# Expert outputs added by indirect DMA into a DRAM table of token sums, the last block applied on TensorE, and the second expert's rows gathered behind the first layer

## What is computed

```python
def moe_ffn(h, router_w, router_b, w1, b1, w2, b2):
    logits = (ht @ router_w + router_b)
    top_val, top_idx = lax.top_k(logits, TOP_K)            # TOP_K = 4
    gates = jax.nn.softmax(top_val, axis=-1)
    ...
    def expert_block(args):                                # 128 slots of one expert
        idx, e = args
        u = clamped_swiglu(h_pad[idx] @ w1[e] + b1[e])
        return u @ w2[e] + b2[e]
    y = jnp.zeros((t + 1, d)).at[slot_tok].add(y_slots * slot_gate[:, None])

ffn = moe_ffn(h, ...)
x = layer_norm(DEEPNORM_ALPHA * x + (1.0 + gt2) * ffn, ln2_g, ln2_b)
```

## Time and profile before

| | us |
|---|---|
| median of 3 runs (2186.21 to 2190.55) | 2189.36 |
| the profiled execution's own time | 2179.64 |
| its span | 2178.0 |
| PE busy, share of the span | 1948.8 (89%) |
| DVE busy | 1630.3 (75%) |
| ACT busy | 1244.0 (57%) |
| POOL busy | 322.9 (15%) |
| mean granted TensorE clock, share of full speed | 0.928 |

### The profile page before, as it was taken

How to read it: one execution, slowest core, us unless ns; L and a number is a source line. 1 busy time by engine, 2 the same in 40 slices (tenths; PEclk the granted TensorE clock), 3 DMA queues, 4 the chain that set the end, 5 groups by cost and what they waited for, 6 DMA issues and landing times.

```text
span 2178.0 us, 26817 instructions
## 1 busy us (share of the span) xinstructions
PE 1948.8 (89%) x9142; PEld 1544.9 (71%) x9142; DVE 1630.3 (75%) x1652; ACT 1244.0 (57%) x1255; POOL 322.9 (15%) x291
## 2 busy tenths in 40 slices
PE   7999888889853798888999999999999999999965
PEld 5766655666641687686888888888888888888851
DVE  5664344853568736777899999999899999999847
ACT  5545555323342132236777777777777777777731
POOL 3436431000000140032000000000000000000012
PEclk9999989989986688978999999999999999999985
DMA  7448423232000101359999999999999999999953
GB/s 207 150 154 271 143 92 122 75 93 58 15 11 0 30 20 47 143 166 323 394 394 389 386 393 382 400 382 400 381 396 388 387 397 381 399 381 400 385 183 128
DMA packets 189918, 536.09 MB, mean 246 GB/s; under 512 B 36146, under 2 KB 60290, under 8 KB 189858
## 3 DMA queue, kind: packets, MB, share of 16 engines
q1 hardware_dynamic: 165506, 461.66, 57.1%
q0 software_dynamic: 17664, 56.86, 7.6%
q10 hardware_dynamic: 6688, 16.79, 1.9%
HBM read 504.92 MB, written 30.33 MB: 246 GB/s over the span
## 4 chain that ended last, share of the span: by engine, by line
PE 52%; DVE 2%; DMA 1%; ACT 0%; issue 0%; POOL 0%; SPq 0%; ACTq 0%; POOLq 0%; DVEq 0%
PE banks L3259 48%; PE banks L3247 2%; PE banks L3323 1%; DMA bias_rows<-bias_parts 1%; PE banks L3253 0%; DVE expert_weights L3516 0%; DMA expert_weights<-slot_outputs,token_slots 0%; DVE x_tokens L3541 0%; DVE out_stats L3526 0%; DVE glu L3516 0%; PE banks L3357 0%; PE banks L3358 0%; ACT weights_hi L3560 0%; DVE expert_weights L3523 0%; DVE expert_weights L3521 0%
## 5 line engine op out<-in xcount | busy, mean ns | idle before, releaser
L3367 DVE TENSOR_TENSOR weights_lo<-expert_weights,weights_hi 128x2048 fp32r<-128x2048 f32 x384 | 878.8, 2290 | 94.6 <-ACT weights_hi L3560 93.7
L3560 ACT ACTIVATE weights_hi<-expert_weights 128x2048 fp32r<-128x2048 f32 x384 | 737.6, 1922 | 227.5 <-PE banks L3259 224.3
L3259 PE MATMUL banks<-weights_hi,rows_hi 128*128 128x512 f32 x1024 | 320.3, 394 | 0.0
L3259 PE MATMUL banks<-weights_hi,rows_lo 128*128 128x512 f32 x1024 | 317.2, 391 | 0.0
L3259 PE MATMUL banks<-weights_lo,rows_hi 128*128 128x512 f32 x1024 | 275.1, 391 | 0.0
L3259 PEld LDWEIGHTS banks<-weights_hi,rows_hi 128*128 128x128 f32 x1024 | 190.7, 189 | 45.5 <-issue 7.5
L3259 PEld LDWEIGHTS banks<-weights_lo,rows_hi 128*128 128x128 f32 x1024 | 192.9, 188 | 40.7
L3259 PEld LDWEIGHTS banks<-weights_hi,rows_lo 128*128 128x128 f32 x1024 | 192.8, 188 | 40.4
L3259 PE MATMUL banks<-weights_hi,u_hi 128*128 128x512 f32 x512 | 161.5, 397 | 3.7 <-ACT weights_hi L3560 3.7
L3259 PE MATMUL banks<-weights_hi,u_lo 128*128 128x512 f32 x512 | 158.8, 392 | 0.0
L3217 POOL DMA_DIRECT2D block_tokens<-slot_tokens x31 | 17.4, 562 | 823.5 <-PE banks L3247 817.2
(11 more groups left out here) (567 smaller groups left out, 2800.4 us busy)
## 6 DMA issues: line engine op xcount, KB each, us to landing
expert_weights<-in_exp_w SPq DMA_DIRECT2D x384, 1024.0 KB, 8.4
enter_rows<-in_ada_w POOLq DMA_DIRECT2D x24, 1024.0 KB, 5.7
slot_outputs<-h_mix ACTq DMA_DIRECT2D x32, 512.0 KB, 7.4
slot_outputs<-zeros SPq DMA_DIRECT2D x4, 1920.0 KB, 10.0
w_in_landing<-in_w_in SPq DMA_DIRECT2D x16, 384.0 KB, 3.4
second_landing<-in_w_in SPq DMA_DIRECT2D x12, 512.0 KB, 3.6
x_tokens<-in_x SPq DMA_DIRECT2D x8, 512.0 KB, 6.8
w_in_landing<-in_w_in SPq DMA_DIRECT2D x8, 512.0 KB, 3.7
```

The source lines that it names most:

```text
L3259: last = nc.tensor.matmul(c.banks[:, bank + n, :], left[:, 2 * q + kk, :], right[:, q, kk * FF + n * 512:kk * FF + (n + 1) * 512], start=s ...
L3367: nc.vector.tensor_tensor(w_lo[:, ch % SPLIT, :], c.raw[:, ch % RAW, :], w_hi[:, ch % SPLIT, :], ALU.subtract).then_inc(lo_ready.sem, 1)
L3560: nc.scalar.activation(w_hi[:, ch % SPLIT, :], c.raw[:, ch % RAW, :], ACT.Copy).then_inc(hi_ready.sem, 1)
```

## The change

Nothing of the arithmetic of an expert is altered. What is:

1. **Token sums in DRAM.** A DRAM table `token_sums` (640 rows: 512 tokens, 128 rows for unused slots) starts with ALPHA times the residual row, stored in "leave" by SP, tile by tile; the ALPHA is put into the norm's gain and shift rows. Each finished block is scaled on DVE by its slot's gate and by (1 + gt2) (`put_y`, one SCALAR_TENSOR_TENSOR from PSUM), and POOL adds it by an indirect DMA with `compute_op=add` into the rows of its tokens (`add_rows`). The store from ACT is gone.
2. **Slot table of pairs.** The slot table now holds a token and its gate (`slot_pairs`, 8 bytes for each slot), and POOL fetches the pair of block b as well (`fetch_pair`). The large zero fill of `slot_outputs` is replaced by two small fills of unused rows.
3. **The last block on TensorE.** Its output stays in SBUF (`ysb`) and is multiplied into the token tiles by matrices made in advance from the gates (`weigh_last`, `turn_last_gates`). The second-layer bias goes into the same PSUM banks (`bias_2`).
4. **The end.** SP loads the four tiles of sums once the last addition has landed; DVE adds PSUM and sums with a running total (one instruction), centres, and applies gain and shift; ACT takes the squares. The 16 gathers, the gate products, the bn_stats and POOL's additions are gone.
5. **The start.** `first_rows(1)` and the first layer's copy of its rows are moved behind expert 0's first layer; `first_rows(0)` is taken over in two halves; `schedule` stands in expert 1's part.

```diff
+                def add_rows(b):
+                    pool.wait_ge(y_taken.sem, 2 + b)
+                    pool.sem_inc(fetches.sem, 1)
+                    nc.gpsimd.indirect_dma_start(sums, bass.IndirectOffsetOnAxis(pair[:, 0:1], 0), ysb, None,
+                                                 compute_op=ALU.add).then_inc(y_added.sem, 16)
                 def step(i):
-
+                    add_rows(i - 2)
                     pool.wait_ge(turned_x.sem, 1 + i)
                     fetch(i + 1)
-
-                further(pool, step, lambda i: pool.wait_ge(y_stored.sem, 32 + i * 16))
-                for t in range(TT):
-                    for k in range(TOPK):
-                        nc.gpsimd.indirect_dma_start(gathered[t][k], None, Y,
-                                                     bass.IndirectOffsetOnAxis(slots[:, t, k:k + 1], 0)).then_inc(came[t].sem, 16)
+                    pool.wait_ge(y_added.sem, i * 16 - 16)
+                    fetch_pair(i - 1)
...
+                def put_y(b, finished):
+                    dve.wait_ge(used.sem, finished)
+                    dve.wait_ge(pair_in.sem, 16 + b * 16)
+                    nc.vector.scalar_tensor_tensor(out=ysb, in0=y_bank, scalar=pair_f[:, 1:2], in1=vec[:, 2, :],
+                                                   op0=ALU.mult, op1=ALU.mult).then_inc(y_taken.sem, 1)
...
                 def step(i):
                     s0 = first_chunk(i)
                     for k in range(4):
                         low(k, s0 + k)
+                    put_y(i - 2, s0)
                     low_u(i - 1)
...
-                first_rows(1, second_bank)
-                pe.wait_ge(c.pool_ready.sem, c.pool_ready.at(1))
-                pe.sem_inc(y_taken.sem, 1)
                 first_layer(0, 0, False)
-                turn_own_u(0)
+                pe.wait_ge(gates_copied.sem, 1)
+                first_rows(1, second_bank)
+                pe.wait_ge(u_ready.sem, 2)
+                turn(first_u, turned_u)
...
+                def last(i):
+                    bias_2((0, 1))
+                    second_layer(pe.snap(i + 1), i * 12 + 8)
+                    bias_2((2,))
+                    pe.wait_ge(last_y.sem, 2)
+                    for t in range(TT):
+                        if t == TT - 1:
+                            bias_2((t,))
+                        for n in range(2):
+                            done = nc.tensor.matmul(c.banks[:, 2 * t + n, :], last_gates_T[:, t, :], ysb[:, n * 512:(n + 1) * 512],
+                                                    start=False, stop=True)
+                        done.then_inc(tile_sums.sem, 1)
...
+                def sum_rows(t):
+                    dve.wait_ge(came[t].sem, 16)
+                    dve.wait_ge(tile_sums.sem, t + 1)
+                    c.dve(dve, v.tensor_tensor_reduce(out=c.x[:, t, :], in0=row_sums(t), in1=c.x[:, t, :], scale=1.0, scalar=0.0,
+                                                      op0=ALU.add, op1=ALU.add, accum_out=row_total[:, t:t + 1]))
```

More of the change, by code:

```diff
@@ L1526, in joined @@
     landed = [own(f"weights_{i}_in", 16) for i in range(RAWS)]
-    x_in, rows_stored, router_in = [own(f"x_{t}_in", 16) for t in range(TT)], own("rows_stored", 16), own("router_in", 16)
+    x_in, kept, router_in = [own(f"x_{t}_in", 16) for t in range(TT)], own("tiles_kept"), own("router_in", 16)
     w_hi, w_lo, y_turned, y_hi, y_lo = own("weights_high"), own("weights_low"), own("y_turned"), own("y_high"), own("y_low")
@@ L3001, in rwkv_core, with mixed @@
         c.masks.passed(1)
-def mixed(c, A, h, part, final, bias2, rb):
+def mixed(c, A, h, h_rows, sums, part, final, bias2, rb):
     nc = c.nc
-    h_rows = nc.dram_tensor("h_rows", [SEQ, D], F32).ap()
     with ExitStack() as ctx:
@@ L3036, in load_expert_chunk, with experts @@
                      src.rearrange("o p k n -> p (o k) n")).then_inc(c.landed[ch].sem, 16)
-def experts(c, A, h, h_rows, bias_rows, Y, gates, slots, plan, vec, out, gates_T, bias2, gate_diag, rb, done_with):
+def experts(c, A, h, h_rows, bias_rows, sums, gates, slots, plan, vec, out, gates_T, bias2, rb, done_with):
     nc = c.nc
@@ L3103, in experts, with further @@
         gates_ready, gates_turned, gates_copied = own("gates_ready"), own("gates_turned"), own("gates_copied")
-        first_scaled, summed, var_ready, root_ready, rstd_ready = (own("first_rows_scaled"), own("tile_summed"), own("variance_ready"),
-                                                                   own("root_ready"), own("rstd_ready"))
-        centred, gained, shifted = own("tile_normalised"), own("tile_gained"), own("tile_shifted")
+        last_ready, last_turned, last_copied = own("last_gates_ready"), own("last_gates_turned"), own("last_gates_copied")
+        last_y, tile_sums, totals, roots, finished = (own("last_y_copied"), own("tile_sums"), own("tile_totals"), own("roots"),
+                                                      own("tiles_finished"))
         def first_chunk(i):
             return i * 12 - 4
-        def further(engine, step, last, start=1):
-            with engine.Fori(start, E) as i:
+        def further(engine, step, last):
+            with engine.Fori(2, E) as i:
                 step(i)
@@ L3426, in own_rows @@
                 def own_rows():
+                    dve.wait_ge(c.sums_stored.sem, 16 * TT)
                     dve.wait_ge(ranks.sem, 1)
@@ L3481, in _ @@
                 low(7, 7)
-                product(0, 0, False)
-                linear(0, 1, 0)
-                product(0, 1, False)
-                low_rows(1, second_bank)
+                dve.wait_ge(c.rows_stored.sem, 16 * TT)
+                product(0, 0, False, first_u)
+                s0 = first_chunk(1)
+                for k in range(3):
+                    low(k, s0 + k)
+                linear(0, 1, 0)
+                product(0, 1, False, first_u)
+                low(3, s0 + 3)
+                low_first_rows(1, second_bank, 0)
+                low_first_rows(1, second_bank, 1)
+                low_u(0)
+                weigh_last()
+                for k in range(4, 7):
+                    low(k, s0 + k)
+                linear(1, 0, s0)
+                low(7, s0 + 7)
+                product(1, 0, True)
+                schedule()
+                for k in range(8, 11):
+                    low(k, s0 + k)
+                linear(1, 1, s0)
+                low(11, s0 + 11)
+                product(1, 1, True)
+                low_rows(2)
+                prepare_rows()
                 def step(i):
@@ L3504, in last, with finish_rows @@
+                def finish_rows(t):
+                    dve.wait_ge(roots.sem, t + 1)
+                    c.dve(dve, v.reciprocal(inverse[:, t:t + 1], inverse[:, t:t + 1]))
+                    v.scalar_tensor_tensor(out=c.x[:, t, :], in0=centred[t], scalar=inverse[:, t:t + 1], in1=vec[:, 1, :],
+                                           op0=ALU.mult, op1=ALU.add).then_inc(finished.sem, 1)
                 def last(i):
+                    for k in range(3):
+                        low(8 + k, i * 12 + 8 + k)
+                    put_y(i - 1, first_chunk(i) + 12)
@@ L3543, in _ @@
-                dve.wait_ge(c.final_loaded.sem, c.final_loaded.at(4))
-                for t in range(TT):
-                    sum_rows(t)
-                    if t >= 1:
-                        gain(t - 1)
-                    finish_rstd(t)
-                gain(TT - 1)
-                dve.wait_ge(gained.sem, TT)
-                nc.vector.tensor_tensor(c.x[:, TT - 1, :], c.x[:, TT - 1, :], vec[:, 1, :], ALU.add).then_inc(summed.sem, 1)
+                    low(11, i * 12 + 11)
+                    dve.wait_ge(used.sem, i * 12 + 12)
@@ L3614, in step @@
                         high(k, s0 + k, landed(k, i), True)
-                    if any_y:
-                        put_y(i - 2, s0)
                     high_u(i - 1)
-                    for k in range(4, 7):
+                    for k in range(4, 8):
                         high(k, s0 + k, landed(k, i), True)
-                    high(7, s0 + 7, landed(7, i), True)
                     silu(i, 0, True)
```

338 lines of the change are left out of this document (190 added, 148 removed).

## The result

| | before | after |
|---|---|---|
| median of 20 runs, us | 2186.72 (2176.32 to 2195.22) | 2200.70 (2182.03 to 2216.22) |
| ratio, 95% interval | 1 | 1.0059 (1.0037 to 1.0081) |
| profiled execution, us (span) | 2179.64 (2178.0) | 2182.03 (2180.4) |

The ratio leaves out one run of the changed kernel, the one of 2216.22, because it is over 1.5% above the fastest. The change makes the kernel 14 us slower, which is 0.6% and clear of the noise. The forecast was 81 us slower (2270): the sign is right, the size is not.

A forecast was written before the change was run, and what follows sets the result against it. TensorE was taken to bound the kernel until 2089 us, then a serial end. Gains of 46 (end) and 8 (start) against 135 lost in the loop gave +81: 2261 profiled, 2270 median, range 2150 to 2375.

The forecast's parts named there:

- The end: After the last turning of u: the span's remaining 89.2 us falls to 43.0, 46 gained.
- The mechanism of the loop: On POOL the fetch waits behind y and the addition, numbers queue behind it, TensorE waits for gathered rows; 135 us lost.
- the size of the chain: In the loop, y out to TensorE's wake: 21.1 us in series against 17.5 available, a wait of 3.6.
- clock's loss: In the loop, TensorE's granted clock falls after a wait of 3.6; half of 1.7 counted, 0.85 us a step.
- lead until the addition's first packet: In the loop's chain, end of the addition's issue to its first packet: 2.4 to 3.2 us, taken as 2.8.
- the half share: In the loop, the gather's transfer at about half share of the DMA engines takes 3.1 us; the addition's 4.3 taken.
- the new small operations: DVE's new small operations, with `schedule` in expert 1's part, would cost 1 or 2 us once cover is gone.
- The start: Ahead of the turning of block 2's rows: half of the row picking moves, 8 us gained (4 to 9).
- hide most of the bias load's wait: At the start, the other 8.4 us of picking fill the 3.68 gap and hide most of a 5.10 wait.
- Queued, but less contended: Rival in the loop: first packets come sooner, chain 19.0, step 36.5, no clock fall, 2181 us; chance 0.17.
- The addition doubled: Rival in the loop: addition at twice the gather's price, transfer 6.2, step 42.2 with the clock, 2351 us; chance 0.19.
- The DMA engines were not the bound: Rival in the loop: 0.5 MB more read makes DMA the bound, step at most 36.3, 2174; 0.20 shared with not queued.

The follow-up runs named there:

- the version with the fetch first: Changed kernel with two lines of GpSimd's step exchanged: the gather of block i+1's rows asked for ahead of block i-2's addition; 2137.9 us, ratio 0.9784.
- The plain write: Changed kernel with the addition replaced by a plain indirect write of the same 512 KB to the same rows; 2164.36 us, ratio 0.9924.
- with the numbers ahead: Changed kernel with only the load of block i+1's token numbers ahead of the addition, the gather still behind it; 2140.88 us, ratio 0.9797.
- without the addition: Changed kernel with the addition's DMA left out, GpSimd's wait for y kept; 2135.48 us, ratio 0.9797.
- The two experiments on the start: Fetch-first kernel with expert 0's second-half first-layer work ahead of expert 1's parts: 2135.0 us; then also block 1's row halves ahead of the fourth chunk: 2136.98 us.

## Why the prediction was right in sign and wrong in size

**The end** was right: 48.5 gained for 46. TensorE's first tile is done 20.75 after the last turning of u, for 20.4; DVE's row work runs at the durations of the earlier trace rows and ends at 37.7, for 37.3; and the additions had landed, as argued. The 2.5 of difference lie behind DVE's last instruction, where 5.7 was kept and 3.1 measured. One term was off and had no weight: the second layer took 12.6, not 10.9, at a granted clock of 0.69 between 2144 and 2149. **The mechanism of the loop** was right too: y is out 1493.95 - 1476.45 = 17.5 after the turning, as the prediction put it; the numbers queue behind the addition; the releaser of TensorE's idle is the gather. What failed is **the size of the chain**, a sum of eight terms of which only the excess over 17.5 counts:

| term | forecast | measured |
|---|---|---|
| GpSimd wakes | 0.7 | 0.8 |
| addition's issue | 1.8 | 1.6 |
| from its end to its first packet | 2.8 | 1.6 |
| transfer 4.3, numbers 2.1 | 6.4 | 5.7 |
| GpSimd wakes | 0.9 | 0.8 |
| gather | 8.4 | 8.44 |
| TensorE wakes | 0.1 | 0.04 |
| sum | 21.1 | 19.07 |
| clock's loss | 0.85 | none seen (clock 1.00) |

The chain is 10% shorter than forecast, but what counts is its excess over 17.5: 3.6 was forecast and 1.57 came, of which TensorE stands idle for 1.35. Times 30 that is about 61 of the 87 us by which the loop was forecast too high; the clock's loss, 30 x 0.85, is the rest. The term that was mis-sized most is the **lead until the addition's first packet**, 2.8 for 1.6. The changed kernel's queues from 1496 to 1498 and from 1498 to 1502 (packets, MB, share of 16 engines) put it at 1498, where the issue had ended at 1494.76 + 1.63 = 1496.4:

```profile
q0 software_dynamic: 1, 0.00, 3.0%
```

```profile
q0 software_dynamic: 151, 0.50, 70.9%
```

The prediction read the earlier trace rows rightly. In half-microsecond windows the gather's first packets of that step stand in 1494.5 to 1495 (the first line below), 3 after the end of its issue. What failed is carrying this lead over to the addition. GpSimd waits behind a gather, but behind the addition it issues the numbers at once. In the version with the fetch first it waits behind the addition too, and there the addition's first packets come as late as a gather's, 4.75 to 5.0 after the start of its issue (the two lines below it, the window from 1275.5 to 1276), not 2.3 to 3.3 as in the seven steps looked at in the changed kernel:

```profile
q0 software_dynamic: 3, 0.01, 16.4%
```

```profile
1270.82 1.65 POOL L3248 DMA_INDIRECT token_sums<-h_mix,block_pairs  x1 [8.87 <-DVE h_mix L3456]
```

```profile
q0 software_dynamic: 16, 0.07, 65.4%
```

The plain write with the numbers right behind it starts as early (2.8 to 3.5), and an addition behind which the gather is issued 2 later lies between (3.8 to 4.8). So in these traces an indirect DMA that another follows on GpSimd's queue starts up to 2 sooner than one that GpSimd waits behind; why it does is not shown.

That the numbers are issued 1.05 after the addition, inside its issue of 1.63, is not what shortened the chain if they land behind its packets, and no run separates the two.

From 1498 to 1502 the addition's queue takes 71% of the engines, not the half share that the prediction gave it. The Trainium skill ("Collectives: The Full Stack", The bandwidth ceiling: the fold count and why AG ≠ RS ≠ AR) says of a ReduceScatter that its add, which reads two sources through one ring, brings it to about half the rate of a plain copy. These traces agree for the indirect addition: about 2.8 of engine time against about 1.36. The prediction took 4.3 for the wall time of the transfer; at 71% of the engines 2.8 is 3.9, so this term was nearly right.

The **clock's loss** depends on the wait and went with it: behind the loop's waits of 1.3 the granted clock is 1.00. Its size, half of 1.7 for a wait of 3.6, was a guess, and too low. The second trace of the changed kernel has one wait close to it, and the clock over the 10 us from 1824 on:

```profile
1824.25 1.41 PE L3267 MATMUL banks<-ident,h_mix 128*128 128x128 f32 x8 [3.76 <-DMA h_mix<-h_rows,block_tokens]
```

```profile
1824.00:1834.00 10.00, 9.75 (x40) 8.15 (x41) 5.00 (x4) 4.46 (x3) 0.57 (x1) 0.83 0.87 343
```

From there to the turning of u it is 13.48, where it is 11.85 behind a wait of 1.3: 1.6 lost, and 2.7 behind waits of 6.4. With a chain as long as forecast, the step would by this row have been about 38.6 + 1.6 = 40.2, not 39.5. A further 0.2 of each waiting step (35.2 without the wait, for 34.97) shows neither as a wait nor in the clock; its cause is open.

Per step the forecast was 4.5 and the loss is 47.9 / 30 = 1.6, of which 0.45 is one event, the first step: TensorE waited 10.6 there and then lost another 2.7. Against an ordinary step three things are later. The gather's issue took 6.93 us on GpSimd, not 1.6. The numbers landed 1.1 later. And y is out 3.0 later: GpSimd starts 1051.78 - 1030.44 = 21.3 after the turning, not 18.3. There VectorE is busy almost without a gap from 1025 on, with `schedule` and the new small operations that the prediction priced at 1 or 2 once their cover was gone. That this makes y late was not tested. The late y is there in all six traces of the changed code that were read for it; the long issue came in the second trace (6.78), with the plain write (8.21) and, with the numbers ahead, at 5.83 with no wait of TensorE; with the fetch first this issue took 1.00, without the addition 1.45. The cause of the long issue is open.

**The start** was wrong: 8 forecast, 1.2 measured. Expert 0's first layer does start where it was forecast, at 968.4 with routing 4.2 later; the loss lies behind it. Half of the picking did move and its 7.30 do lie ahead of the turning of u, but the step "hide most of the bias load's wait" assumed that everything else was ready. VectorE and ScalarE work in the order written, and there the second half of expert 0's first-layer result stands behind the parts of expert 1's chunks, which had not landed. The row of ScalarE, and what TensorE waited for then:

```profile
991.72 1.91 ACT L3654 ACTIVATE weights_hi<-expert_weights 128x2048 fp32r<-128x2048 f32 x1 [2.70 <-DMA expert_weights<-in_exp_w]
```

```profile
1000.92 1.97 PE L3267 MATMUL banks<-ident,x_tokens 128*128 128x128 f32 x8 [2.98 <-DVE x_tokens L3429]
1005.50 0.62 PE L3273 MATMUL banks<-bias_rows,ones_bf 3*128 3x512 bf16 x4 [2.60 <-issue]
```

The two experiments on the start show that 4.5 of the missing 6.8 come back by order alone.

**The rivals.** "Queued, but less contended", with a step of 36.5 and no fall of the clock, was the nearest in the loop: its sum is 19.0, for 19.07. That is in part luck. Its first packet at 2.4 and its gather at 7.9 were 1.6 and 8.4, and its reason, a less loaded stream, is not what shortened the lead. Its total of 2181 stands for the median, which came at 2200.7; for the profiled execution it is 2179.6 - 8 = 2172, where 2182 came, and most of these ten us are the start's missing 6.8 and the 4.2 ahead of routing. "The addition doubled" was right on the engine time and wrong on the path. The DMA engines were not the bound, yet they would have been with 0.5 MB more.

## What to carry over

When a chain of DMAs just exceeds a loop's period, forecast its excess, not its length: an error of 10% in the sum was a factor of more than 2 in the excess, and more in the time, because in this loop the clock's loss came with the longer waits. Take the price of a DMA from a row in which the same thing follows it on its queue. Ask of each wait that is added on an idle engine what the queue behind it feeds: the order of two lines made 63 us (2200.7 against 2137.9), and with the better order the addition cost the loop nothing. Work that is moved to fill a gap helps only if what ends the gap is ready; in-order engines may hold it behind loads of a later stage.

## What the runs showed that was not expected

- An indirect adding write of 512 KB costs the DMA engines about 2.8 us, a plain one about 1.36, but what queues behind it lands only 1.5 later.
- The next DMA of GpSimd's queue starts 1.05 into an addition's issue of 1.63, and the addition's first packets come 2.3 to 3.3 after its start then, but 4.75 to 5.0 where GpSimd waits behind it.
- Two traces of the same code differ by 12 us ahead of the experts, by TensorE's granted clock in two stretches (0.89 or 0.80 from 300 to 360, 0.99 or 0.91 from 780 to 840).
- At 395 GB/s one more write of 512 KB a step costs 1.0 us a step even when no chain waits for it, while the addition itself cost nothing in the version with the fetch first (loop of 1061.1, against 1061.4 in the kernel before, which stored the same bytes by another queue).
